# Moving one bank copy and two operand loads ahead of a weight split at the end of a projection

## The reference

```
h = rms_norm(x) @ w_in            # 2048 x 8192, split into b, c, h, z
u = c * h
y = (b * conv3_causal(u) * silu(z)) @ w_out     # 2048 x 2048
x = x + y
```

## Time and profile before

| | |
|---|---|
| median of 3 runs (lowest, highest) | 2417.43 us (2414.26, 2418.49) |
| the profiled execution's own time | 2417.12 us |
| its span, first to last instruction | 2415.2 us |
| mean granted TensorE clock | 0.991 of full |
| PE busy (matmuls) | 2344.8 us, 97% |
| DVE busy | 1677.2 us, 69% |
| ACT busy | 1232.2 us, 51% |
| mean rate of all transfers | 236 GB/s |

### The profile page before, as it was taken

The page is one execution under the profiler, slowest core; times in us unless marked ns, Lnnn a source line. Parts: engine busy times, 40 slices in busy tenths (PEclk is TensorE's granted clock), DMA queues, the critical chain, the costliest instruction groups (busy, mean ns, idle before and its releaser), DMA issues.

```text
span 2415.2 us, 49410 instructions
## 1 busy us (share of the span) xinstructions
PE 2344.8 (97%) x20029; PEld 2043.9 (85%) x20029; DVE 1677.2 (69%) x1981; ACT 1232.2 (51%) x2216; POOL 110.8 (5%) x69
## 2 busy tenths in 40 slices
PE   7999999999998998999999999999999989899998
PEld 6999999999998998999999999999999633355555
DVE  7988878878877883555898878777767567533311
ACT  5544444444444546767555577776555345421111
POOL 4000000000000120000000000000000023200000
PEclk9999999999999999999999999999999999999999
DMA  6344344344358674334677777788888999999998
GB/s 212 105 129 122 105 137 130 106 137 131 120 172 294 205 232 158 100 119 162 227 267 270 250 255 258 271 278 289 283 296 297 332 378 422 360 373 377 390 405 305
DMA packets 383173, 571.00 MB, mean 236 GB/s; under 512 B 19513, under 2 KB 304690, under 8 KB 363698
## 3 DMA queue, kind: packets, MB, share of 16 engines
q1 hardware_dynamic: 305858, 461.55, 55.4%
q10 hardware_dynamic: 76960, 106.03, 12.2%
q0 software_dynamic: 128, 0.26, 0.0%
HBM read 508.24 MB, written 59.54 MB: 235 GB/s over the span
## 4 chain that ended last, share of the span: by engine, by line
PE 85%; DMA 5%; DVE 5%; ACT 3%; issue 2%; POOL 0%; ACTq 0%; SPq 0%; DVEq 0%; POOLq 0%
PE psum L1144 21%; PE psum L1813 19%; PE psum L1148 11%; PE psum L1821 9%; PE psum L2519 8%; PE psum L1864 5%; PE psum L2598 4%; DMA left<-in_w_out_a_dram 2%; PE psum L2577 1%; PE psum L1829 1%; PE psum L2558 1%; DMA w_raw<-in_w_kv_dram 1%; DVE h_keys_turned L1755 1%; DMA w_raw<-in_w_in_b_dram 1%; ACT w_raw L1576 1%
## 5 line engine op out<-in xcount | busy, mean ns | idle before, releaser
L1813 PE MATMUL psum<-x_hi,w_hi 128*128 128x272 f32 x2048 | 435.3, 294 | 6.7 <-DMA x_lo<-x_split_scratch 4.1
L1813 PE MATMUL psum<-x_lo,w_hi 128*128 128x272 f32 x2048 | 426.4, 289 | 0.0
L483 ACT ACTIVATE left_rounded<-left 128x1024 fp32r<-128x1024 f32 x273 | 287.8, 1056 | 185.2 <-PE psum L1148 172.0
L800 DVE TENSOR_TENSOR left_rounded<-left,left_rounded 128x1024 fp32r<-128x1024 f32 x273 | 334.0, 1227 | 23.0 <-ACT left_rounded L483 22.6
L1144 PE MATMUL psum<-right_a_rounded,left_rounded 128*128 128x272 f32 x2496 | 343.3, 290 | 6.5 <-DVE work L1053 4.1
L1813 PEld LDWEIGHTS psum<-x_hi,w_hi 128*128 128x128 f32 x2048 | 322.8, 190 | 24.0 <-issue 19.4
L1144 PEld LDWEIGHTS psum<-right_a_rounded,left_rounded 128*128 128x128 f32 x2496 | 326.9, 190 | 7.1 <-issue 7.1
L1813 PEld LDWEIGHTS psum<-x_lo,w_hi 128*128 128x128 f32 x2048 | 322.6, 189 | 0.0
L1755 DVE STREAM_TRANSPOSE h_keys_turned<-h_ring 128x1024 f32<-128x1024 f32 x256 | 299.9, 1215 | 19.3 <-PE psum L1864 11.1
L1821 PE MATMUL psum<-x_hi,w_lo 128*128 128x272 f32 x2048 | 284.5, 294 | 0.0
L1821 PEld LDWEIGHTS psum<-x_hi,w_lo 128*128 128x128 f32 x2048 | 264.2, 188 | 8.5 <-issue 4.7
(11 more groups left out here) (273 smaller groups left out, 2798.4 us busy)
## 6 DMA issues: line engine op xcount, KB each, us to landing
h_ring<-in_cache_k_dram SPq DMA_DIRECT2D x256, 512.0 KB, 6.2
ring<-in_cache_v_dram SPq DMA_DIRECT2D x128, 1024.0 KB, 7.9
left<-in_w_in_a_dram SPq DMA_DIRECT2D x128, 512.0 KB, 4.0
w_raw<-in_w_kv_dram SPq DMA_DIRECT2D x16, 2048.0 KB, 12.9
w_raw<-in_w_in_b_dram SPq DMA_DIRECT2D x15, 2048.0 KB, 9.1
left<-in_w_out_a_dram SPq DMA_DIRECT2D x32, 512.0 KB, 5.8
wo_raw<-in_w_out_b_dram SPq DMA_DIRECT2D x32, 512.0 KB, 8.4
ring<-in_w_out_b_dram SPq DMA_DIRECT2D x16, 1024.0 KB, 6.3
```

What stands on the lines that cost most here:

```text
L483: act.activation(arena.left_high(q), arena.left(LEFT[mm], n), ACT.Copy).then_inc(hi_ready, 1)
L800: dve.tensor_tensor(arena.left_low(name, n), arena.left(name, n), arena.left_high(q).bitcast(F32), ALU.subtract).then_inc(lo_ready, 1)
L1813: pe.matmul(psum[n % 2][:, g, 0:GT], m.WH[n % 2][:, k * P:(k + 1) * P], x[:, k * T + g * GT:k * T + (g + 1) * GT], start=(k == 0 and x is ...
```

## The change

```
@@ conv_extras on ScalarE
-                if n == IN_STEPS - 1 and mm:
+                if n == IN_STEPS - 1 and mm in (1, 2, 3, 6):
                     load_right(mm - 1)
@@ the loop over q on ScalarE
                     take_quarter(n)
                 if mm == 5:
                     take_u3(n)
-                split_high(q + 3)
+                if n == IN_STEPS - 1 and mm in (4, 5):
+                    load_right(mm - 1)
+                    if mm == 5:
+                        split_high(q + 2)
+                        split_high(q + 3)
+                else:
+                    split_high(q + 3)
```

## The result

The change makes the kernel slower by 0.34%: median 2424.14 us (7 runs, 2423.39 to 2428.20) against 2416.46 (7 runs, 2414.26 to 2418.57) for the kernel before in the same comparison, ratio 1.0034 with a 95% interval of 1.0025 to 1.0044. That is +7.7 us by the medians, and 6.0 to 10.6 us by the interval; forecast were +9.8 and a median of 2427, with a range of 2421 to 2431. The profiled execution took 2424.48 us, its span is 2422.5.

A forecast was written before the change was run, and what follows sets the result against it. PE was taken to bound the kernel (85% of the chain). The terms 10.95 - 1.44 + 0.3 = +9.8 us on 2417.1 gave 2426.9, forecast as a median of 2427 us, range 2421 to 2431.

The forecast's parts named there:

- A11 and the first stop: Before product 31.6: the 5.05 us PE stop stays, as the gather waits behind L778 for that weight block; value 0.
- A12: Weight block of step 32 lands 11.0 us late; PE's stop before 32.0's last pair grows by 10.95 us.
- The wait before 32.6: PE's 1.44 us stop ahead of product 32.6 goes: -1.44 us, bounds 0 to -1.44.
- The clock: Slow 1.2 GHz stretch of PE after the long stop, on the rest of 32.0 and 32.1: +0.3 us, bounds 0 to +1.7.
- The sum: Whole kernel: 10.95 - 1.44 + 0.3 = +9.8 us, forecast median 2427 us.
- A: q1 sends several small packets per turn, so step 32's block lands by about 730: 2414.9 us, chance 0.06.
- B: The copy releases 31.6 at once and its 5.05 us stop goes: 2410.8 us, chance 0.03.
- C: Step 32's block is delayed by less than half, as q10 still gets a hole: +4 us, 2421, chance 0.08.
- D: Long stop costs two slow stretches and the 1.44 us before 32.6 stay: 2430, up to 2431.5 us, chance 0.08.

The follow-up runs named there:

- e1: Kernel before with only the bank copy take_u3 moved ahead of the split of 32.0, both loads left behind it; 2416.19 us, ratio 1.0005.
- g_after_gather_first: Full change plus sum_2(32) put behind the gather on DVE in step 31; 2423.74 us, ratio 1.0033 to the kernel before.
- e3: Kernel before with only load_right(3) moved ahead of the split of 32.0; 2424.96 us, ratio 1.0035.
- before_again: The kernel before, unchanged, run once more for a second profile; 2415.56 us.
- e4: Full change, with sum_4(32) and the split of 32.3 behind last_right(0) and (1); 2416.84 us, ratio 1.0001 to the kernel before.
- h_copies_first: Kernel before with take_u3 ahead of the splits of 32.0 and 33.0, loads unmoved, several sums and the split of 32.3 later; 2408.85 us, ratio 0.9974.
- e2: Kernel before with only load_right(3) and (4) moved ahead of the split of 32.0, copy left behind it; 2424.78 us, ratio 1.0033.

## Why the prediction was right

**A11 and the first stop.** Forecast: nothing changes, since the gather stands behind L778. Measured: 5.11 for 5.05 us. It is shown from both sides, by e1 (copy alone: the stop stays) and by g_after_gather_first (gather freed as well: the stop goes).

**A12.** Forecast: issue to landing near 26 us, 10.95 us later than before. Measured: 26.13 us, and L798 starts 745.72 - 733.56 - 0.94 = 11.2 us later. Both ways of counting it held: equal packets in both queues until q10 is nearly dry, and q10 nearly dry from 744. e3 shows that it is the closed hole and not the number of early loads. PE resumes 4.69 us after L798 starts (750.41 - 745.72), as before.

**The wait before 32.6.** Forecast -1.44. From 32.2 to 32.6 PE took 769.51 - 757.47 = 12.04 us against 757.83 - 744.11 = 13.72 (32.2 started at 744.11 before), so -1.68. One reading ahead of it was off without harm: blocks A21 and A22 of step 33 were forecast to land at 752 to 753 again, but landed at 747.2 and 748.8, since both were queued behind A12 when the hole opened. The price itself rested on one profile. From 32.2 to 33.0, the slow stretch behind the stop included, PE needed 16.8 us before, 21.2 in before_again and 18.4 in e1, against 15.1 in both profiles of the changed kernel: what goes away is 1.7 to 6.2 us, not 1.44.

**The clock.** Forecast +0.3, bounds 0 to 1.7. From 32.0's last pair to 32.2: 757.47 - 750.41 = 7.06 us against 744.11 - 738.25 = 5.86, so +1.2, because 1.2 GHz lasted until 756.5. 31.6 ran slowly for longer too (5.51 us against 4.34), under the wait for A12, which is why the stop itself was 12.4 and not 13.3 us.

**The sum.** 11.2 - 1.7 + 1.2 = +10.7 us, and 769.51 - 757.83 - 0.94 = 10.7. At the seam of this pair the forecast of 9.8 was a little low. Against the medians, +7.7, it was a little high, and inside the interval of 6.0 to 10.6. What was mis-sized is that one profile stood for the kernel. From 31.5 to 32.2, where 10.95 + 0.3 were forecast, the first pair of profiles shows +12.4 and the second +13.5 us; from 32.2 to 33.0, where -1.44 was forecast, they show -1.7 and -6.2. That makes 10.7 and 7.3 us for the seam. A cost and a gain were both forecast too small, and that the sum still came so near is in part luck. The mean of 9.0 from two profiles of each cannot be told apart from 7.7.

**The rivals.** A (q1 sends several packets in a turn) is refuted by the counts and by A12's 26.1 us. The prediction says that A would win by the rule of the Trainium skill in "DMA: Bandwidth & Descriptors", section "Queues, rings and completion order". That does not follow: turns of several rows in both queues leave the counts equal and A12 starved. B (31.6 released by the copy) falls with e1. C (A12 delayed by less than half) falls with 26.2 us in three variants. D's second slow stretch came in part (+1.2 us); its other term, the stop before 32.6, did not stay.

## What to carry to other kernels

Before moving a transfer forward, look at what shares the engines with it: a queue of small packets beside one of large packets gets its turns but hardly any bytes, and may be living from the moments in which the other queue is empty. Before moving an instruction that releases a wait, walk every engine between it and the waiting one; here the same block held two of them, and freeing one was worth nothing. Where an in-order engine waits for a block, put what needs it last, behind everything that is ready (e4, h_copies_first).

## What the runs showed of the hardware

- While both queues had work, they moved one packet record for one, whatever their sizes: 118 to 118 with 512 against 7616 bytes, 198 to 196 with 512 against 3264 to 4352. A load of 1024 packets of 512 bytes took 17.1 us beside a q10 full of the first kind, and 26.1 us when it also had to stand behind another such load.
- SP was held in one issue for 7.6 us when two of its blocks were still under way. With two under way it took 10.2 us in the changed kernel and 11.7 in g_after_gather_first (one of the two issues near 729). In these three traces the next issue started 2.6 us or more after the held one ended.
- After its long stop PE ran at 1.2 GHz for 6.1 us of work in the changed kernel (stop of 12.4 us), but for 3.9, 3.6 and 3.1 us in e2, e3 and g_after_gather_first (stops of 13.4, 13.5 and 19.5 us). After the first stop, of 5.1 us in both, it did so for 2.8 us in the profile of before and for 5.4 in that of the changed kernel. The length of the slow stretch did not follow the length of the stop.
